# Rotary queries of the latent attention: products and turnings between the latent queries and among the first attention blocks

## The chip, the cores and the metric

One core of a Trainium2 chip runs one program. The metric is the device time of one execution in microseconds (us), the median over the runs of a kernel. TensorE is called PE in the profile (its weight loads PEld), VectorE DVE, ScalarE ACT, GpSimd POOL and SyncE SP. Each engine works off its own instructions in order, and they meet through semaphores.

## The reference, cut to what matters

The program is one step of a two-layer decoder trunk for 512 prompt tokens and 8 sample tokens. Layer 0 mixes tokens by sliding-window attention and retention, layer 1 by multi-head latent attention; behind each stand a cross-attention into 256 memory tokens and a mixture of experts. The change touches layer 1's latent attention alone:

```python
def mla_project(x, pos, w_in, q_norm, kv_norm, w_uq, w_uk):
    cq, ckv, kr = jnp.split(x @ w_in, [MLA_Q_RANK, MLA_Q_RANK + MLA_KV_RANK], axis=-1)
    cq = rms_norm(cq, q_norm)
    ckv = rms_norm(ckv, kv_norm)
    kr = rope(kr[:, :, None, :], pos)[:, :, 0]
    q = (cq @ w_uq).reshape(B, S, MLA_HEADS, MLA_NOPE + MLA_ROPE)      # 8 heads, 64 + 32
    q_nope, q_rope = jnp.split(q, [MLA_NOPE], axis=-1)
    q_rope = rope(q_rope, pos)
    q_lat = jnp.einsum('bshn,chn->bshc', q_nope, w_uk)                 # 128 per head
...
def mla_attend(q_lat, q_rope, rows, mask):
    s = einsum('bqhc,bkc->bhqk', q_lat, ckv) + einsum('bqhr,bkr->bhqk', q_rope, kr)
    s = jnp.where(mask, s * ((MLA_NOPE + MLA_ROPE) ** -0.5), NEG_INF)
    p = jax.nn.softmax(s, axis=-1)
    return jnp.einsum('bhqk,bkc->bqhc', p, ckv)
```

## The kernel before, in words

The 520 tokens are five tiles of rows: four of 128 prompt tokens, and the 8 sample tokens as tile 4. Layer 1's latent attention is `latent_attention`, which stands once for each engine (PE line 1737, ACT 2316, DVE 3099).

PSUM is cut into four pairs of banks, and all that PE makes goes through them. `psum_jobs` (line 257) writes the order of all jobs out by hand; job n uses pair n modulo 4. `open_` makes PE wait until the job four places earlier has been read out (`free`); `close` tells the reader that a job is full, `full` waits for that, and `taken` waits until a job has been read out. So every job that is put into the order shifts which earlier readout each later job waits for.

The jobs of the stretch are these. `qn` j: the plain queries of two heads by feature (line 1776), read out by DVE (even j) or ACT (odd j). `qrope` t: the rotary part of all heads for tile t (line 1793, four matmul records); DVE turns it by position in `rotate` (lines 3113 to 3118, and 3121, 3122 for tile 4), which reads PSUM with its first three instructions. `qrT` t: PE turns the rotated tile back to features (line 1803; line 1806 for tile 4), and ACT reads it out (line 1986, the helper `copy`) into `qrT2`, or for tile 4 with four small copies. `ql` h: the latent query of head h over all 520 tokens (line 1059), read out by DVE (even h) or ACT (odd h).

The order before is `qrope` 0, `ql` 0 to 7, then `qrope` 1, `qrT` 0, `qrope` 2, `qrT` 1, and so on to `qrT` 4. PE then waits until `qrT` 4 and `ql` 6 and 7 have been read out, and starts the attention.

Attention runs in 16 blocks: block i is prompt tile i // 4 (keys 128 times (i // 4 + 1)) and two heads. Each block has three PSUM jobs: S, the scores (lines 1830 and 1833), T, the probabilities turned (line 1082), and O, the probabilities times the latents (line 1840). `latent_steps` (line 156) gives PE's order S0, S1, then S(i+2), T(i), O(i-1). DVE's order is the maxima of block i+1 (lines 2494, 2495, 2502), then the scaling of the probabilities of block i (2513, 2516), then, from block 6 on, an unrelated piece on `x` (3142). ACT's order is the exponentials of block i+1 (2097), then the readouts of T(i) and O(i-1) (1986). T(i) needs the scaled probabilities of block i; O(i) needs T(i) read out. Sample tokens have their own attention behind block 15: it begins with 16 transposes (line 1852) of cached pages that SP and POOL have loaded meanwhile (lines 657, 658).

Of the kernel before, what the change touches and what calls it, by code (L numbers as in the profile page):

```python
# [34 lines left out]
NT = 5  # L35
# [30 lines left out]
def tile_cols(t):  # L66
    return slice(t * P, t * P + ROWS[t])
# [177 lines left out]
LATENT_PE = [*LATENT_IN[:-2], ("qn", 0), ("oinT", 3), ("qn", 1), ("oinT", 4)]  # L245


LATENT_GROUPS = [slice(0, P), slice(P, 2 * P), slice(2 * P, 3 * P), slice(3 * P, 416)]
LATENT_ROWS = {2: [0], 3: [1], 4: [2, 3, 4]}
LAST_TILES = [4, 0, 1, 2, 3]  # L250
# [6 lines left out]
def psum_jobs():  # L257

    jobs = []
    jobs += [("xT", -1, t) for t in range(NT)]  # L260
    jobs += [("qa", j) for j in range(4)] + [("ka",), ("va",)]
    jobs += [("kaTok",), ("qr", 0)]
    for step, i in sliding_steps(len(SWA_BLOCKS)):
        jobs += SWA_WEAVE[i] if step == "W" else [("swa" + step, i)]
    jobs += SWA_SAMPLE
    for n in range(4):
        jobs += [("retS", n), ("retK", n)] + RET_WEAVE.get(("K", n), [])
        jobs += [("retO", n), ("retU", n)] + RET_WEAVE.get(("U", n), [])
        if n:
            jobs += [("retG", n - 1)]  # L270
    for l in range(DEPTH):
        if l == 1:
            jobs += LATENT_PE
            jobs += [("qn", j) for j in (2, 3)]
            jobs += [("qrope", 0)]
            jobs += [("ql", h) for h in range(8)]
            for t in range(NT):
                jobs += ([("qrope", t)] if t else []) + ([("qrT", t - 1)] if t else [])
            jobs += [("qrT", 4)]
            jobs += [("mla" + s, i) for s, i in latent_steps(len(MLA_BLOCKS))]  # L280
            jobs += [("pkT", 0), ("pkT", 1), ("pN",)] + [key for key in PAGE_PE if key[0] != "row"]
            jobs += [("uv", j) for j in range(4)]
        jobs += [memory_job(l, *key) for key in MEM_PE[l] if key[0] != "ms2" and (key[0] != "rt" or key == ("rt", 0))]
        if l == 0:
            jobs += [("memF", 1, 0), ("memF", 1, 1), ("rank", 0), ("mkv", 1, 0), ("table", 0), ("mkv", 1, 1)]
        else:
            jobs += [("rank", 1), ("table", 1)]
        for s, b in block_order():
            jobs += [("moe" + s, l, b)] + ([("mkT", 1)] if (l, s, b) == (0, "H", 0) else [])
    jobs += [("cmb", t) for t in LAST_TILES]  # L290
    return jobs


def decoder_step(nc, io, outs):
# [78 lines left out]
    with ExitStack() as ctx:  # L373
# [217 lines left out]
        def pair(key):  # L591
            return PS[:, J[key] % 4, :]
# [10 lines left out]
        def taken(eng, key):  # L603

            n = J[key]
            eng.wait_ge(pair_free[n % 4], n // 4 + 1)
# [421 lines left out]
        def _(pe):  # L1028
# [708 lines left out]
            def latent_attention():  # L1737
# [51 lines left out]
                def q_rope(t):  # L1789
                    key = ("qrope", t)  # L1790
                    o = open_(key)
                    for k in range(2):
                        mm = pe.matmul(o[0:ROWS[t], 0:256], cqT[:, k, tile_cols(t)], uq[:, k, 512:768],
                                       start=(k == 0), stop=(k == 1))
                    close(mm, key)

                def q_rope_back(t):
                    key = ("qrT", t)
                    o = open_(key)
                    pe.wait_ge(s["qrtok_ready"], t + 1)  # L1800
                    if t < 4:
                        for c in range(2):
                            mm = pe.transpose(o[:, c * P:c * P + P], qr_tok[:, t % 2, c * P:c * P + P], ident[:, :])
                    else:
                        for h in range(8):
                            mm = pe.transpose(o[:, 8 * h:8 * h + 8], qr_rep[0:8, h, :], ident[0:8, 0:8])
                    close(mm, key)

                q_rope(0)
                taken(pe, ("ukT",))  # L1810
                taken(pe, ("qn", 2))
                taken(pe, ("qn", 3))
                for h in range(8):
                    key = ("ql", h)
                    open_(key)
                    b, c = 64 * (h % 2), h // 2
                    close(by_feature(key, lambda k: ukT[b:b + 64, c, :], lambda k: qnT[b:b + 64, c, :], 1), key)
                for t in range(1, NT):
                    q_rope(t)
                    q_rope_back(t - 1)  # L1820
                q_rope_back(4)
                taken(pe, ("qrT", 4))
                taken(pe, ("ql", 6))
                taken(pe, ("ql", 7))

                def score(i, o, blk):
                    n, h0, g, w = blk
                    o = o.rearrange("p (g w) -> p g w", g=g)
                    for h in range(h0, h0 + g):
                        pe.matmul(o[:, h - h0, 0:w], q_lat[:, h, n * P:n * P + P], ckvT[:, 0:w], start=True, stop=False)  # L1830
                    for h in range(h0, h0 + g):
                        b, c = 32 * (h % 4), h // 4
                        mm = pe.matmul(o[:, h - h0, 0:w], qrT2[b:b + 32, c, n * P:n * P + P], krT4[b:b + 32, 0:w],
                                       start=False, stop=True, **({"tile_position": (b, 0)} if b == 96 else {}))
                    return mm
# [4 lines left out]
                        mm = pe.matmul(o[:, 0:g * P], rows[:, c, 0:P], v[:, c, :, :], start=(c == 0), stop=(c == n))  # L1840
                    return mm

                attention("mla", score, apply, latent_steps(len(MLA_BLOCKS)))


                for signal, count in (("pages_in", SP_REQUESTS), ("late_pages_in", DB - SP_REQUESTS)):
# [137 lines left out]
        def _(act):  # L1984
# [3 lines left out]
            def take(key, dst, src):  # L1988
                full(act, key)
                free(copy(dst, src(pair(key)) if callable(src) else src), key)  # L1990
# [139 lines left out]
                    between(i + 1)  # L2130
                    outputs(i)

            def latent_blocks():
                exps, probs_turned, outputs = attention_steps("mla")
                n = len(MLA_BLOCKS)
                exps(0)
                for i in range(n):
                    if i + 1 < n:
                        exps(i + 1)
                    probs_turned(i)  # L2140
                    if i:
                        outputs(i - 1)
                outputs(n - 1)

            n_rows = [0]
# [170 lines left out]
            def latent_attention():  # L2316
# [44 lines left out]
                for h in (1, 3, 5, 7):  # L2361
                    take(("ql", h), halves(q_lat[:, h, :]), halves)
                for t in range(4):
                    take(("qrT", t), qrT2[:, :, tile_cols(t)], lambda o: o[:, 0:256].rearrange("p (c q) -> p c q", c=2))

                taken(act, ("ql", 6))
                taken(act, ("ql", 7))
                act.wait_ge(s["qrS_zero"], 1)
                copy(qlS[:, :, 0:8], q_lat[:, :, 512:520].rearrange("p h b -> p b h"))
                full(act, ("qrT", 4))  # L2370
                for q in range(4):
                    ins = copy(qrS[32 * q:32 * q + 32, q, :, 0:8], pair(("qrT", 4))[32 * q:32 * q + 32, 0:64].rearrange("p (h b) -> p b h", h=8))
                free(ins, ("qrT", 4))

                act.wait_ge(s["moe_done"], 1)
                latent_blocks()
# [48 lines left out]
        def _(dve):  # L2425
# [673 lines left out]
            def latent_attention():  # L3099
# [31 lines left out]
                rotate(0)  # L3131
                for h in (0, 2, 4, 6):
                    take(("ql", h), halves(q_lat[:, h, :]), halves(pair(("ql", h))))
                for t in range(1, NT):
                    rotate(t)
                def gains(i):
                    if i == GAIN_BLOCKS:
                        dve.wait_ge(s["ln_in"], 32 * 3)
                    if i >= GAIN_BLOCKS:
                        t, c = divmod(i - GAIN_BLOCKS, 2)  # L3140
                        xt = x[0:ROWS[t], t, :]
                        ins = dve.tensor_tensor(xt, xt, lnb[0:ROWS[t], c, :], (ALU.mult, ALU.add)[c])
                        if c:
                            ins.then_inc(s["x_ready"], 1)
                        else:
                            link(ins)
# [93 lines left out]
```

## Time and profile before

| | us |
|---|---|
| median of 3 runs | 1076.29 |
| lowest and highest | 1073.14, 1077.27 |
| the profiled execution | 1078.72 |
| its span | 1077.1 |
| PE busy | 973.2 (90%) |
| DVE, ACT, POOL busy | 525.6, 353.5, 254.1 |
| mean granted TensorE clock | 0.941 |

The profiled execution is 1.62 us longer than its span and 2.43 us above the median of the three runs. Durations below are of that one execution. PEclk in the profile is the granted clock of TensorE as a share of full speed; it has two levels, 0.50 (1.2 GHz) and 1.00 (2.4 GHz), and a stretch that holds both shows a value between. A matmul's record includes its way through the array, so records overlap, and what one costs PE is better read from start to start, or in the chain of waits, which cuts the overlap off.

### The profile page before, as it was taken

The numbers are of one execution on the slowest core, as the hardware profiler recorded it, in microseconds if no ns is written. First come the engines' busy times: TensorE is split into PE (matmuls) and PEld (weight loads), VectorE is DVE, ScalarE is ACT, GpSimd is POOL, SyncE is SP. The second block draws the span as 40 slices with busy tenths as digits, with TensorE's granted clock in tenths as the row PEclk, the third lists the DMA queues.
The fourth block names the chain that finished last, engine by engine and source line by source line (L and its number), as shares of the span: only waits on it lengthen the run. The fifth ranks groups of instructions, "written<-read, shape, count | busy, mean of one in ns | idle before, by whom it ended". The sixth has DMA issues, their size and how long they took to land.

```text
span 1077.1 us, 17831 instructions
## 1 busy us (share of the span) xinstructions
PE 973.2 (90%) x6998; PEld 602.9 (56%) x6998; DVE 525.6 (49%) x1070; ACT 353.5 (33%) x879; POOL 254.1 (24%) x281
## 2 busy tenths in 40 slices
PE   7978999998999998899999298899799986999995
PEld 6866788887445857633333166657548663333332
DVE  0345630466648667243223464685268673433327
ACT  2325432120001523333333243455314342333423
POOL 2220710042500001445410115600000015362121
PEclk9998999989899998999999699899999986999998
DMA  9422361172206244989998603441056136999978
GB/s 324 108 91 46 89 198 37 42 197 78 69 0 163 79 196 152 400 298 414 415 407 336 223 1 72 100 136 61 21 175 274 40 133 215 334 398 402 417 234 196
DMA packets 81612, 203.73 MB, mean 189 GB/s; under 512 B 22682, under 2 KB 47938, under 8 KB 72432
## 3 DMA queue, kind: packets, MB, share of 16 engines
q1 hardware_dynamic: 61568, 153.44, 39.5%
q0 software_dynamic: 19952, 49.05, 14.8%
q8 instruction: 60, 0.98, 0.4%
q14 instruction: 32, 0.26, 0.1%
HBM read 184.46 MB, written 25.92 MB: 195 GB/s over the span
## 4 chain that ended last, share of the span: by engine, by line
PE 75%; DVE 11%; DMA 6%; ACT 4%; issue 3%; POOL 1%; SPq 0%; DVEq 0%; POOLq 0%; ACTq 0%
PE PS L1613 14%; PE PS L1421 11%; PE PS L1059 9%; PE PS L1160 6%; PE PS L1628 5%; PE PS L1444 3%; PE PS L1124 3%; PE PS L1047 2%; ACT arena L1986 2%; DMA x<-y_tok 2%; PE PS L1082 2%; PE PS L1830 2%; DMA arena<-in_moe_w_in_dram 2%; PE PS L1755 2%; PE PS L1840 2%
## 5 line engine op out<-in xcount | busy, mean ns | idle before, releaser
L1986 ACT ACTIVATE arena<-PS 32x520 f32<-32x520 f32 (+9 forms) x150 | 74.0, 505 | 188.0 <-PE PS L1059 42.4
L1613 PE MATMUL PS<-ring,arena 128*32 128x512 f32 x648 | 116.9, 592 | 2.9 <-DMA arena<-in_moe_w_in_dram 1.5
L1613 PE MATMUL PS<-arena 128*32 128x512 f32 x648 | 111.1, 602 | 2.9 <-issue 1.8
L1059 PE MATMUL PS<-xT,ring 128*128 128x260 f32 x416 | 94.6, 388 | 3.1 <-DVE arena L2455 2.3
L3048 DVE COPY arena<-PS 128x256 f32<-128x256 f32 x24 | 10.2, 425 | 171.6 <-PE PS L1621 171.6
L1059 PEld LDWEIGHTS PS<-xT,ring 128*128 128x128 f32 x416 | 79.0, 192 | 18.0 <-DVE arena L2455 4.3
L826 POOL TENSOR_TENSOR rstd<-rstd,small 128x1 f32<-128x1 f32 (+1 forms) x25 | 16.3, 652 | 272.4 <-DVE rstd L2743 245.3
L2263 ACT ACTIVATE arena<-PS,lnc 128x128 f32<-128x128 f32 x192 | 69.6, 470 | 22.9 <-PE PS L1602 22.9
L1628 PE MATMUL PS<-ring,arena 128*32 128x512 f32 x432 | 69.0, 595 | 1.2 <-DVE arena L3048 1.2
L1160 PE MATMUL PS<-ring,xT 128*128 128x256 f32 (+2 forms) x336 | 65.1, 354 | 0.0
L1047 PE MATMUL PS<-ident,x 128*128 128x128 f32 (+1 forms) x240 | 39.2, 318 | 28.0 <-DVE x L2819 20.0
L1613 PEld LDWEIGHTS PS<-arena 128*32 128x32 f32 x648 | 30.4, 111 | 60.4 <-issue 56.3
L864 POOL DMA_INDIRECT y_tok<-arena,slot_dest x22 | 22.3, 1014 | 174.4 <-ACT arena L2291 168.5
L1160 PEld LDWEIGHTS PS<-ring,xT 128*128 128x128 f32 (+1 forms) x336 | 57.0, 186 | 7.0
L1613 PEld LDWEIGHTS PS<-ring,arena 128*32 128x32 f32 x648 | 31.5, 110 | 48.8 <-issue 44.6
L1421 PE MATMUL PS<-ring,xT 128*128 128x512 f32 x128 | 56.8, 593 | 0.7 <-ACT xT L1986 0.7
L2281 ACT ACTIVATE arena<-PS 128x256 f32<-128x256 f32 x24 | 9.3, 386 | 142.9 <-PE PS L1613 142.9
L1995 ACT ACTIVATE xT<-PS,lnc 128x128 f32<-128x128 f32 (+1 forms) x100 | 37.7, 438 | 54.7 <-PE PS L1047 35.6
L1047 PEld LDWEIGHTS PS<-ident,x 128*128 128x128 f32 (+1 forms) x240 | 35.0, 202 | 36.8 <-issue 33.3
L1613 PE MATMUL PS<-xT,arena 128*32 128x512 f32 x240 | 50.3, 593 | 0.8 <-DVE arena L3032 0.8
L1421 PE MATMUL PS<-ring,arena 128*128 128x512 f32 x96 | 48.1, 643 | 2.1 <-issue 2.1
L2097 ACT ACTIVATE pbuf<-PS,negmax 128x256 f32<-128x256 f32 (+3 forms) x96 | 45.1, 481 | 10.7 <-DVE negmax L2502 10.6
(433 smaller groups left out, 1867.9 us busy)
## 6 DMA issues: line engine op xcount, KB each, us to landing
arena<-in_moe_w_in_dram SPq DMA_DIRECT2D x27, 1024.0 KB
ring<-in_moe_w_in_dram SPq DMA_DIRECT2D x27, 1024.0 KB
ring<-in_moe_w_out_dram SPq DMA_DIRECT2D x18, 1024.0 KB
ring<-in_w_in_even_dram SPq DMA_DIRECT2D x11, 1024.0 KB
xT<-in_moe_w_in_dram SPq DMA_DIRECT2D x10, 1024.0 KB
arena<-in_moe_w_out_dram SPq DMA_DIRECT2D x8, 1024.0 KB
xT<-in_moe_w_out_dram SPq DMA_DIRECT2D x6, 1024.0 KB
y_tok<-in_c_zeros_dram POOLq DMA_DIRECT2D x8, 512.0 KB, 10.6
```

Of the source, the lines that this page charges most:

```text
L1047: mm = pe.transpose(o[:, chunk_cols(k, r)], by_k[:, k, :], ident[0:r, 0:r])
L1059: mm = pe.matmul(o[out_rows, 512 * h:512 * h + HALF], lhs(k), rhs(k)[:, HALF * h:HALF * h + HALF], start=(k == 0), stop=(k == nk - 1))
L1124: mm = pe.matmul(o[:, 512 * c:512 * c + 256], memF[l][:, k, m * P:m * P + P], wview(("m" + w, l))[:, k, :], start=(k == 0), stop=(k == KD ...
L1160: mm = pe.matmul(o[0:ROWS[t], n * width:n * width + width], xT[:, k, tile_cols(t)], w[:, k, cols], start=(k == 0), stop=(k == KD - 1))
L1421: mm = pe.matmul(o[0:ROWS[t], 512 * h:512 * h + 512], out_part(i, 2 * n + k, t), w[:, k, 512 * h:512 * h + 512], start=(n == 0 and k == 0) ...
L1444: mm = pe.matmul(o[:, j * r:j * r + r], w[:, k, j * P:j * P + P], xT[:, k, tile_cols(t)], start=(k == 0), stop=(k == KD - 1))
L1613: mm = pe.matmul(o[group(q), 0:512], xT_[:, k, group(q)], w(q, k), start=(k == 0), stop=(k == KD - 1), **quarter(q))
L1628: mm = pe.matmul(o[group(q), 512 * h:512 * h + 512], a[:, c, group(q)], w(q)[:, c, 512 * h:512 * h + 512], start=(c == 0), stop=(c == 1), ...
L1986: return act.activation(dst, src, ACT.Copy)
L1995: ins = act.activation(dst(k), src(k), ACT.Identity, scale=lnc[:, i, 0, k:k + 1], bias=lnc[:, i, 1, k:k + 1])
L2097: ins = act.activation(prob_view(kind, i)[:, h, :], score_view(kind, i)[:, h, :], ACT.Exp, bias=negmax[:, n % 2, h:h + 1], scale=SCALE[kin ...
L2263: ins = act.activation(dst[:, k, :], o[:, k * P:k * P + P], ACT.Identity, scale=lnc[:, 3 * l + 1, 0, k:k + 1], bias=lnc[:, 3 * l + 1, 1, k ...
```

## The change

PE, DVE and ACT get a new order by hand, and the order of PSUM jobs follows it. `qrope` 1, `qrT` 0, `qrope` 2 and `qrT` 1 stand between the `ql` jobs. `qrope` 3 stands behind S1, `qrT` 2 behind S2, `qrope` 4 (the sample rows) behind O0, `qrT` 3 behind O1, and `qrT` 4 behind O3. DVE rotates tile 3 behind the scaling of block 0 and tile 4 behind that of block 2. ACT reads out `qrT` 2, 3 and 4 at the end of its blocks 0, 2 and 4. A block waits for the `qrT` of its own tile where that tile's first block begins, and no longer for `qrT` 4. The work itself is the same, instruction for instruction.

```diff
+LATENT_QUERY = keys("qrope.0 ql.0 ql.1 qrope.1 ql.2 ql.3 qrT.0 ql.4 ql.5 qrope.2 qrT.1 ql.6 ql.7")
+LATENT_QUERY_DVE = keys("rot.0 ql.0 ql.2 rot.1 ql.4 rot.2 ql.6")
+LATENT_QUERY_ACT = keys("ql.1 ql.3 qrT.0 ql.5 qrT.1 ql.7")
+MLA_WEAVE = {("S", 1): [("qrope", 3)], ("S", 2): [("qrT", 2)], ("O", 0): [("qrope", 4)], ("O", 1): [("qrT", 3)], ("O", 3): [("qrT", 4)]}
+MLA_WEAVE_DVE = {0: 3, 2: 4}
+MLA_WEAVE_ACT = {0: 2, 2: 3, 4: 4}
...
-            jobs += [("qrope", 0)]
-            jobs += [("ql", h) for h in range(8)]
-            for t in range(NT):
-                jobs += ([("qrope", t)] if t else []) + ([("qrT", t - 1)] if t else [])
-            jobs += [("qrT", 4)]
-            jobs += [("mla" + s, i) for s, i in latent_steps(len(MLA_BLOCKS))]
+            jobs += LATENT_QUERY
+            for s, i in latent_steps(len(MLA_BLOCKS)):
+                jobs += [("mla" + s, i)] + MLA_WEAVE.get((s, i), [])
...
-                for t in range(1, NT):
-                    q_rope(t)
-                    q_rope_back(t - 1)
-                q_rope_back(4)
-                taken(pe, ("qrT", 4))
+                for key in LATENT_QUERY:
+                    if key == ("ql", 0):
...
+                    steps[key[0]](*key[1:])
                 taken(pe, ("ql", 6))
                 taken(pe, ("ql", 7))
...
+                    if h0 == 0:
+                        taken(pe, ("qrT", n))
...
+                for st_, i in latent_steps(len(MLA_BLOCKS)):
+                    mla[st_](i)
+                    for key in MLA_WEAVE.get((st_, i), []):
+                        steps[key[0]](*key[1:])
...
+                latent_blocks(lambda i: turned_queries(MLA_WEAVE_ACT[i]) if i in MLA_WEAVE_ACT else None)
...
                 def gains(i):
+                    if i in MLA_WEAVE_DVE:
+                        rotate(MLA_WEAVE_DVE[i])
```

## Rows read from the trace of the kernel before

**Rows 1.** The page, part 1: busy time of each engine over the whole span.

```profile
PE 973.2 (90%) x6998; PEld 602.9 (56%) x6998; DVE 525.6 (49%) x1070; ACT 353.5 (33%) x879; POOL 254.1 (24%) x281
```

**Rows 2.** Chain that ended last, 600 to 780 us: start us, us, what.

```profile
664.35 0.86 PE PS L1793 x4
665.24 4.08 PE PS L1059 x32
...
675.93 0.69 DVE arena L3122
...
677.43 0.21 ACT decay L1986
...
678.38 1.22 PE PS L1830 x4
...
687.79 0.87 PE PS L1830 x4
688.66 0.66 PE PS L1833 x4
...
690.74 1.03 ACT pbuf L2097 x4
...
741.99 1.75 PE PS L1852 x16
```

**Rows 3.** Stretches on PE: us, PE busy (x), PEclk, DMA share, GB/s.

```profile
656.00:661.00 5.00, 4.26 (x16) 0.66 0.47 111
674.00:678.00 4.00, 1.64 (x13) 0.93 0.38 87
678.00:687.00 9.00, 8.62 (x37) 0.50 0.47 98
740.00:750.00 10.00, 10.00 (x86) 1.00 0.28 92
755.00:759.00 4.00, 2.32 (x47) 1.00 0.00 0
```

**Rows 4.** Timeline of PE: start us, us, engine line op, tiles xcount [idle before <-releaser].

```profile
682.14 1.22 PE L1830 MATMUL PS<-arena 128*128 128x128 f32 x4
683.29 0.80 PE L1833 MATMUL PS<-arena 32*128 32x128 f32 x4
684.08 0.66 PE L1082 MATMUL PS<-ident,pbuf 128*128 128x128 f32 x2
684.53 1.06 PE L1830 MATMUL PS<-arena 128*128 128x128 f32 x4
...
689.22 0.44 PE L1082 MATMUL PS<-ident,pbuf 128*128 128x128 f32 x2
689.50 0.60 PE L1840 MATMUL PS<-pT,arena 128*128 128x256 f32 x2
689.93 1.03 PE L1830 MATMUL PS<-arena 128*128 128x256 f32 x4
```

**Rows 5.** Timeline of DVE, the same columns.

```profile
671.81 0.42 DVE L3113 TENSOR_TENSOR arena<-PS,rope_t 128x256 f32<-128x256 f32 x1
...
672.66 0.43 DVE L3118 TENSOR_TENSOR arena<-arena 128x256 f32<-128x256 f32 x1
...
684.14 0.43 DVE L2494 TENSOR_TENSOR PS<-PS,band 128x256 f32<-128x256 f32 x1 [0.20 <-PE PS L1833]
...
685.33 0.48 DVE L2516 TENSOR_SCALAR pbuf<-pbuf,rowsum 128x128 f32<-128x128 f32 x2
...
692.11 0.69 DVE L2495 TENSOR_REDUCE rowmax<-PS 128x2 f32<-128x512 f32 x1
```

**Rows 6.** Timeline of ACT, the same columns.

```profile
683.38 0.37 ACT L2097 ACTIVATE pbuf<-PS,negmax 128x128 f32<-128x128 f32 x1 [1.01 <-DVE negmax L2502]
...
684.00 0.20 ACT L2097 ACTIVATION_READ_ACCUMULATOR pbuf<-PS,negmax 128x1 f32 x1
```

**Rows 7.** Timeline of SP, its DMA queue.

```profile
718.69 0.33 SPq L658 DMA_DIRECT2D xT<-in_cache_mla_dram  x1
```

More of the change, by code:

```diff
@@ L1807, in q_rope_back, with query_latents @@
                     close(mm, key)
[L1809 to L1813, printed above, removed]
+                def query_latents(h):
                     key = ("ql", h)
@@ L1817, in latent_attention @@
                     close(by_feature(key, lambda k: ukT[b:b + 64, c, :], lambda k: qnT[b:b + 64, c, :], 1), key)
-                for t in range(1, NT):
-                    q_rope(t)
-                    q_rope_back(t - 1)
-                q_rope_back(4)
-                taken(pe, ("qrT", 4))
+                steps = {"qrope": q_rope, "qrT": q_rope_back, "ql": query_latents}
+                for key in LATENT_QUERY:
+                    if key == ("ql", 0):
+                        taken(pe, ("ukT",))
+                        taken(pe, ("qn", 2))
+                        taken(pe, ("qn", 3))
+                    steps[key[0]](*key[1:])
                 taken(pe, ("ql", 6))
@@ L1841, in apply @@
                     return mm
-                attention("mla", score, apply, latent_steps(len(MLA_BLOCKS)))
+                mla = attention_steps("mla", score, apply)
+                for st_, i in latent_steps(len(MLA_BLOCKS)):
+                    mla[st_](i)
+                    for key in MLA_WEAVE.get((st_, i), []):
+                        steps[key[0]](*key[1:])
                 for signal, count in (("pages_in", SP_REQUESTS), ("late_pages_in", DB - SP_REQUESTS)):
@@ L2131, in sliding_attention, with latent_blocks @@
                     outputs(i)
-            def latent_blocks():
+            def latent_blocks(between):
                 exps, probs_turned, outputs = attention_steps("mla")
@@ L2142, in latent_blocks @@
                         outputs(i - 1)
+                    between(i)
                 outputs(n - 1)
@@ L2360, in latent_attention, with turned_queries @@
                     take(("qn", j), halves(qnT[:, j, :]), halves)
[L2361 to L2373, printed above, removed]
+                def turned_queries(t):
+                    if t < 4:
+                        take(("qrT", t), qrT2[:, :, tile_cols(t)], lambda o: o[:, 0:256].rearrange("p (c q) -> p c q", c=2))
+                        return
+                    act.wait_ge(s["qrS_zero"], 1)
+                    full(act, ("qrT", 4))
+                    for q in range(4):
+                        ins = copy(qrS[32 * q:32 * q + 32, q, :, 0:8], pair(("qrT", 4))[32 * q:32 * q + 32, 0:64].rearrange("p (h b) -> p b h", h=8))
+                    free(ins, ("qrT", 4))
+                    taken(act, ("ql", 6))
+                    taken(act, ("ql", 7))
+                    copy(qlS[:, :, 0:8], q_lat[:, :, 512:520].rearrange("p h b -> p b h"))
+                for what, n in LATENT_QUERY_ACT:
+                    if what == "qrT":
+                        turned_queries(n)
+                    else:
+                        take(("ql", n), halves(q_lat[:, n, :]), halves)
                 act.wait_ge(s["moe_done"], 1)
-                latent_blocks()
+                latent_blocks(lambda i: turned_queries(MLA_WEAVE_ACT[i]) if i in MLA_WEAVE_ACT else None)
                 for g in range(2):
@@ L3130, in latent_attention @@
                     take(("qn", j), halves(qnT[:, j, :]), halves(pair(("qn", j))))
[L3131 to L3135, printed above, removed]
+                for what, n in LATENT_QUERY_DVE:
+                    if what == "rot":
+                        rotate(n)
+                    else:
+                        take(("ql", n), halves(q_lat[:, n, :]), halves(pair(("ql", n))))
                 def gains(i):
+                    if i in MLA_WEAVE_DVE:
+                        rotate(MLA_WEAVE_DVE[i])
                     if i == GAIN_BLOCKS:
```

## The prediction, made before the changed kernel was run

> **What bounds the kernel.** I read four views, from coarse to fine. Part 1 of the page says which engine fills the span: PE is busy for 90% of it [rows 1], so what counts is PE's own work and the holes in it. The chain of waits says where the edited stretch lies and who releases whom. It runs from the first rotary product at about 664.3 to the first transpose of the sample attention at 741.99 [rows 2], 77.7 us, and nearly all of it is PE. The exception stands ahead of the first block: the eight latent-query products take 4.08 us from 665.24 to 669.3, yet block 0's scores start only at 678.38. The last links are DVE's copy for the sample rows at 675.93, their turning, and ACT's four small copies from 677.43 [rows 2]. The stretches say what that did to the clock: in 674 to 678 PE was busy for 1.64 of 4 us, and after it the granted clock was 0.50 for all of 678 to 687, with PE busy 8.62 of 9 [rows 3]. The timelines of PE, DVE and ACT give the durations of a block's steps [rows 4 to 6]. The reader is to see two costs in the old order, a hole and a slow clock behind it, and to ask what the new order pays for removing them.
>
> **What hole and clock cost now.** From 669.3 to 678.38 are 9.1 us. Four rotary products at 0.89 (one lasts from 664.35 to 665.24 [rows 2]) and some 1.5 for the five turnings are 5.1 of work, so the holes are about 4.0. Moved work costs the same wherever it goes, as PE is the bound. In the new order not all of the hole goes (below).
> At 0.50 a score job of 128 keys takes 1.94 (682.14 to 684.08) [rows 4], 1.88 in the chain's measure. No row shows it at 1.00. Half is 0.94, and a job of 256 keys at 1.00, with twice the columns, takes 1.53 (0.87 and 0.66) [rows 2]; between these I take 1.0, as the columns halve too. Four such jobs then lose 3.5. Two T jobs lose 0.17 each (0.45 against 0.28 from start to start, 684.08 and 689.22 [rows 4]), O0 some 0.4 (0.43 at full clock [rows 4], taken to double), the start of S4 0.1. The slow clock costs 4.4.
> On that price there is a figure in the Trainium skill, TensorE: Matmul & The Clock Gate, section Back-to-back issue gap: about 81 ns for a weight load and matmul of 128 columns at full clock. An estimate by it is 0.65 for the eight records of such a score job, and the result would fall by some 0.3 us. No row here shows that job at full clock.
>
> **What the new order adds.** I walked the three engines through the new order with the rows' durations, each waiting for what the semaphores name, and did so first for the old order: it ended within 0.1 us of the trace. Durations: score 1.0 (128 keys) and 1.53 (256); DVE's maxima and scaling of one block 1.67 (684.14 to 685.81), 0.3 more for 256 keys because the maximum takes 0.69 [rows 5]; exponentials 0.82 (683.38 to 684.20 [rows 6]) and 1.03 [rows 2]; a rotation 1.28 (671.81 to 673.09 [rows 5]), of which PSUM is free after 0.84, and 0.68 more for tile 4 (the copy at 675.93 lasts 0.69 [rows 2]); ACT's copies for the sample rows 0.95 (677.43 to 678.38 [rows 2]) and one more for the sample latents.
> Between the latent queries PE waits twice, 0.8 each. `ql` 4 needs the pair of `qrope` 1, which DVE reads behind `ql` 0 and `ql` 2. S0 needs `ql` 6, which DVE copies behind the rotation of tile 2. So S0 starts at about 673.2 instead of 678.4, with two rotary products and three turnings still to do. Of the 4.0 of holes 1.6 stay: a gain of 2.4. The walk of the old order had only 3.5 of them, since it lets records follow without the small gaps; by it the gain is 1.9, and I take that, the two walks being alike in this.
> Inside the attention the four pairs of PSUM decide. Before, a score job opened when a T or O job was read out. The five added jobs shift this by one place each, and for a while a job has to wait for the exponentials of the latest scores:
> T1 opens when S2 is read out. DVE does the rotation of tile 3 ahead of the maxima of block 2 (its `rotate` is queued behind the scaling of block 0), so scaling 1 and exponentials 2 end near 680.2. PE is done with S3 at 678.9: 1.4 idle.
> S4 needs S3's exponentials, queued on ACT behind T1 and O0: 0.4, partly under `qrope` 4.
> S5 needs S4's exponentials. DVE is in the rotation of tile 4 (1.9 with its copy) until 683.9, then the maxima (1.3), then ACT 1.0: 686.4. PE has only T2, O1 and `qrT` 3 to do meanwhile: 1.6 idle. Here the wait for the sample rows comes back that stood ahead of block 0 before.
> T4: 0.4. S7 needs S6's exponentials, and ACT does T4, O3 and the sample rows' copies first, until 693.3; the exponentials end at 694.3, PE has been idle since 691.9: 2.4.
> With 0.2 at S3 the sum is 6.3, against 0.5 in the same blocks of the old order. From S7 on the pairs fall back into the old pattern, and blocks 8 to 15 cost what they cost.
> The sum, with the clock at 1.00 throughout: minus 1.9, minus 4.4, plus 5.8 is minus 0.5 us.
>
> **Queues it moves past.** Nothing moves on SP or POOL. The last cached page is requested at 718.69 [rows 7], over 20 us before 742, so an attention shorter by some us still doesn't wait for pages. The slot of the rotary weights is released some 15 us later than before, but its next load comes behind the sample attention. DVE's pieces on `x` begin at block 6, behind both rotations. All of these I cost at nothing.
>
> **The clock is the open term.** In 674 to 678 PE was busy 1.64 of 4 us, and the clock fell; in 755 to 759 it was busy 2.32 of 4 and the clock stayed at 1.00 [rows 3]. The new order has no hole as long as the old one but three of 1.4 to 2.4 us close together. Around S7 PE is idle for 2.8 of 4 us, which is nearer to the row where it fell. A single fall is short in this trace: within 656 to 661 the mean of 0.66 makes it 3.4 of the 5 us at 0.50 [rows 3]. If 3.4 us run at half speed, up to half is lost: the walk gives 0.6 where the loss hides under the next hole and 1.9 where it does not, 1.3 in the middle. Added to minus 0.5 that is plus 0.8.
>
> **The rivals.**
> A, the forecast: the holes come as walked and the clock falls once. Plus 0.8 (plus 0.1 to 1.4). Chance 0.45.
> B: the holes come, the clock holds, as at 755 to 759. Minus 0.5. Chance 0.22.
> C: it falls twice, at S5's hole and at S7's. The walk gives 3.5 on minus 0.5: plus 3.0. Chance 0.14.
> D, slower: it falls at T1's hole near 680.5 and doesn't come back before S7, as it stayed low from 678 to 687 though PE was busy [rows 3]. All the work from T1 to S6 runs at half speed, some 6.5 us more: plus 6.1. It decides from the point where the clock is low at S4 and the hole before S5 keeps it low. For it: the stretch holds the same short jobs. Against it: 256-key jobs are denser, and at 687 it came back among them. Chance 0.10. A rule of the Trainium skill speaks for it, same page, section Part 4: PE-mode transpose: the clock's rise doesn't engage for transposes, which don't count as busy in the same way; T and `qrT` jobs would then be holes too. The trace speaks against that rule here, since 740 to 750, mostly transposes, ran at 1.00 [rows 3].
> E, faster: the change does less harm than the pairs' order says, as the exponentials end before PE asks (reads overlap more than the rows let me see). Then the 5.8 shrink towards nothing and the result is minus 6.3. Against it: the old order's walk, with the same durations, fits. Chance 0.05.
> The rest, 0.04, is for a shift further down that none of these name.
>
> **How the numbers follow.** The profiled execution would take 1078.72 + 0.8 = 1079.5. The median of the runs before is 2.4 below that execution, so the time is 1076.29 + 0.8 = 1077.1. The runs of before spread from 3.2 below to 1.0 above their median. For 8 in 10 I take B with that spread downwards, 1076.29 - 0.5 - 2.8 = 1073.0, and C with half its way to D upwards, 1081.5. A measurement of this kernel tells 0.5%, 5.4 us, from no change. A, B and C lie within it, D beyond with some spread of C, E beyond on the other side: faster 0.05, within 0.83, slower 0.12.
>
> **What would show it.** Right: S0 near 673; PE waiting for ACT's exponentials (line 2097) ahead of S5 and S7 by 1.6 and 2.4, and ahead of T1 for DVE or ACT by 1.4; the granted clock at 1.00 from 670 to 680; the first transpose at line 1852 within 1.5 of 742. The forecast is wrong if S7's hole is under 1, if the clock is at 0.50 for more than one short stretch between 673 and 700, or if blocks 8 to 15 take another time than before.

## The result, and the profile after

The kernel before took 1076.2 us (median of 8 runs, 1073.14 to 1081.98), the changed one 1082.95 us (median of 8 runs, 1081.54 to 1087.2). The ratio is 1.0065 with a 95% interval of 1.0047 to 1.0082, so the change costs some 6.8 us (7.0 by the ratio). The forecast was plus 0.8 (no change that can be told), with a range up to 1081.5; the change is slower by a little over the bound of 0.5%, and by more than the range. The profiled execution of the changed kernel took 1087.2 us, its span 1085.5; that of before had a span of 1077.1.

Part 1 of the changed kernel's page answers to [rows 1]. The span grew by 8.4 us, PE's busy time by 3.0 with the same number of records: a part is dearer records, the rest idle time.

```profile
PE 976.2 (90%) x6998; PEld 601.6 (55%) x6998; DVE 524.8 (48%) x1070; ACT 352.1 (32%) x879; POOL 253.4 (23%) x281
```

Next the chain that ended last, of the changed kernel (start us, us, what), which answers to [rows 2]. Its lines are shifted: the rotary products are L1796, the scores L1834 and L1837, the exponentials L2105, the page transposes L1860.

```profile
666.31 0.86 PE PS L1796 x4
...
676.32 0.70 PE PS L1834 x4
...
682.47 0.81 ACT pbuf L2105 x4
...
690.09 1.03 ACT pbuf L2105 x4
...
698.46 1.03 ACT pbuf L2105 x4
...
749.75 1.75 PE PS L1860 x16
```

Before, too, the chain left PE for exponentials behind the start of block 0 (at 690.74 [rows 2], for one), but PE was idle for at most 0.42 us at any such place. Now it leaves PE ahead of T1 (683.33), S5 (691.17) and S7 (699.54), the three places that the walk had named, with PE idle for 1.2 to 2.4 us. PE's timeline gives their size (idle time and what ended it in brackets at the end of a line):

```profile
672.01 1.15 PE L1062 MATMUL PS<-arena 64*128 64x260 f32 x8 [1.14 <-DVE arena L3129]
...
676.32 0.70 PE L1834 MATMUL PS<-arena 128*128 128x128 f32 x4 [0.79 <-DVE arena L3141]
...
677.37 0.71 PE L1834 MATMUL PS<-arena 128*128 128x128 f32 x4
...
683.33 0.69 PE L1085 MATMUL PS<-ident,pbuf 128*128 128x128 f32 x2 [1.17 <-ACT pbuf L2105]
...
691.17 1.13 PE L1834 MATMUL PS<-arena 128*128 128x256 f32 x4 [1.78 <-ACT pbuf L2105]
...
699.54 1.38 PE L1834 MATMUL PS<-arena 128*128 128x256 f32 x4 [2.41 <-ACT pbuf L2105]
```

The stretches on PE of the changed kernel (us, PE busy, PEclk, DMA share, GB/s) answer to [rows 3]:

```profile
678.00:683.00 5.00, 4.15 (x29) 1.00 0.46 103
683.00:687.00 4.00, 3.67 (x10) 0.57 0.41 101
687.00:700.00 13.00, 8.58 (x50) 1.00 0.45 100
700.00:707.00 7.00, 7.00 (x20) 0.52 0.30 64
```

The granted clock is at its upper level (1.00) where before it was at 0.50, but it falls behind T1's hole (0.57 of 4 us, so 3.4 us at the lower level) and again behind S7's (0.52 of 7, so 6.7 us), there with PE busy without a pause. Together that is about the 10 us of before.

To compare all kernels I use one stretch, from the start of the first rotary product in PE's timeline to the start of the first page transpose, and within it the starts of score jobs. "Rest" is all from that transpose to the end of the span. Before and after were profiled again later (below), so before has three traces and after two.

| | S0 after | S7 after | stretch | rest | low clock within it |
|---|---|---|---|---|---|
| before | 14.19 | 30.85 | 77.64 | 335.23 | 10.2 |
| before again | 14.18 | 31.21 | 78.00 | 336.10 | 10.2 |
| before, third | 14.18 | 30.98 | 77.73 | 333.99 | 10.2 |
| after | 10.17 | 33.39 | 83.44 | 335.94 | 3.4 and 6.8 |
| after again | 10.17 | 31.92 | 81.95 | 336.27 | 6.8 |

By the means the stretch grew by 4.9 us (82.7 against 77.8) and the rest by 1.0.

### The profile page after: what moved, and what is told of

Its sections match the earlier page's. It is cut to its first block, busy times and chain, and to the rows that moved or that the text cites. A ratio compares the mean times of both kernels' runs of the same rounds, so it can differ in the third digit from the quotient of the medians.

```text
span 1085.5 us, 17835 instructions
## 1 busy us (share of the span) xinstructions
PE 976.2 (90%) x6998; PEld 601.6 (55%) x6998; DVE 524.8 (48%) x1070; ACT 352.1 (32%) x879; POOL 253.4 (23%) x281
## 4 chain that ended last, share of the span: by engine, by line
PE 75%; DVE 12%; DMA 5%; ACT 4%; issue 3%; POOL 1%; SPq 0%; DVEq 0%; POOLq 0%; ACTq 0%
PE PS L1616 15%; PE PS L1424 11%; PE PS L1062 9%; PE PS L1163 6%; PE PS L1631 6%; PE PS L1447 3%; ACT arena L1994 2%; PE PS L1127 2%; PE PS L1050 2%; DMA arena<-in_moe_w_in_dram 2%; PE PS L1085 2%; PE PS L1758 2%; PE PS L1844 2%; PE PS L1834 2%; PE PS L1605 1%
## 5 line engine op out<-in xcount | busy, mean ns | idle before, releaser
L3062 DVE COPY arena<-PS 128x256 f32<-128x256 f32 x24 | 10.2, 425 | 172.4 <-PE PS L1624 172.4
L2105 ACT ACTIVATE pbuf<-PS,negmax 128x256 f32<-128x256 f32 (+3 forms) x96 | 44.9, 480 | 10.0 <-DVE negmax L2516 9.9
```

Source lines behind the costliest of these rows:

```text
L2105: ins = act.activation(prob_view(kind, i)[:, h, :], score_view(kind, i)[:, h, :], ACT.Exp, bias=negmax[:, n % 2, h:h + 1], scale=SCALE[kin ...
```

## The experiments

The theory to be tested had two parts: the walk through the PSUM pairs is right, so holes of the forecast size come; and the clock's fall behind them costs more than the 1.3 forecast. Its rivals: the two first traces differ by chance, as the clock may fall anywhere (R1); the early rotary products between the latent queries do the harm, not those among the blocks (R2); the holes cost by themselves, the clock little (R3). A further question is which move of the sample rows would bring what the change wanted.

**The same two kernels again.** No edit; one more execution of the changed kernel and two of before, each with its trace.

> The kernel before once more, for a second trace of the stretch from the first rotary product to the last attention block. In the first it took 77.6 us with 10.2 us at 0.50. Theory: the order and the holes are the same to 0.1 us, but where the clock is low is not, as the clock's falls in the four variants so far came at other places behind the same holes; with 3 to 7 us at 0.50 it takes 75 to 76.5. Rival: it is fixed by the program, 77.6 again.

> The kernel before a third time: with the first two traces it shows how far the stretch's length differs from execution to execution. Theory: between 75 and 78 us, by where and how long the clock is low from 677 to 690. Rival: 77.6 each time.

> The changed kernel once more, for a second trace. In the first the stretch took 83.4 us with 10.2 at 0.50, of them 6.8 behind S7's hole. Theory: holes of 1.2, 1.8 and 2.4 us ahead of T1, S5 and S7 again; between 3.4 and 14 us at 0.50, so 80 to 85 us. Rival: 83.4 again, within 0.3.

Measured: 1077.14 and 1075.01 us for before, 1082.48 for the changed kernel, beside 1076.74 (median of 17 runs of before taken with them). The stretches on PE around block 0, before again and then the third trace of before:

```profile
672.00:675.00 3.00, 0.83 (x10) 1.00 0.43 101
675.00:686.00 11.00, 10.46 (x42) 0.53 0.40 97
686.00:698.00 12.00, 11.74 (x60) 1.00 0.41 98
```

```profile
675.00:686.00 11.00, 10.15 (x42) 0.53 0.42 99
```

The low clock behind block 0's hole stays for some 10.3 us (0.53 of 11; 10.2 by finer stretches) in each of three traces, though PE is busy for over 10 of the 11 us. I had expected the other two traces of before to show a stretch of 75 to 76.5, with an earlier return of the clock; that was wrong. R1 falls for this part: the fall here is the same in all three executions. The changed kernel again, timeline and stretches of PE:

```profile
679.75 0.44 PE L1085 MATMUL PS<-ident,pbuf 128*128 128x128 f32 x2 [1.17 <-ACT pbuf L2105]
...
686.13 1.13 PE L1834 MATMUL PS<-arena 128*128 128x256 f32 x4 [1.55 <-ACT pbuf L2105]
...
694.50 1.29 PE L1834 MATMUL PS<-arena 128*128 128x256 f32 x4 [2.41 <-ACT pbuf L2105]
```

```profile
680.00:695.00 15.00, 10.61 (x58) 1.00 0.42 99
695.00:702.00 7.00, 7.00 (x19) 0.52 0.36 83
```

Same holes, same fall behind S7, but none behind T1, though its hole is 1.17 us in both traces. So the fall behind S7 comes in both traces and the one behind T1 in one of them (a kernel below has T1's hole of 1.17 us as well, and the clock holds there too); the latter cost 1.5 us (S7 after 33.39 against 31.92). From S7 to the end of the stretch both traces of the changed kernel take the same, 50.05 and 50.03, and the three of before 46.79, 46.79 and 46.75. The fall behind S7 costs 3.3 us.

**The holes filled.** Unneeded matmuls into an unused part of the open PSUM pair stand where PE would wait. Nothing of the computation is left out.

```diff
+FILLED = {("S", 3): [(("mlaT", 0), 2)], ("O", 1): [(("qrT", 3), 3)], ("O", 3): [(("qrT", 4), 4)]}
+def fill(key, n):
+    for _ in range(n):
+        pe.matmul(pair(key)[:, 512:768], ident[:, :], ckvT[:, 0:256], start=True, stop=True)
...
                         steps[key[0]](*key[1:])
+                    for key, n in FILLED.get((st_, i), []):
+                        fill(key, n)
```

A first kernel had 5, 7 and 9 of them:

> The changed kernel with 21 idle matmuls (128x256, into an unused half of a pair, their results read by nobody) in the three holes ahead of T1 (5), S5 (7) and S7 (9); at some 0.22 us each they are shorter than the holes. Theory P: the holes stay (1.2, 1.8, 2.4 us) but the clock stays at 1.00 from block 0 on; what the two falls cost in the trace (10.2 us at 0.50, some 4.5 to 5 us lost) comes back: 4 to 5 us faster than the changed kernel, +1.5 to +3 on before. A rival (the holes alone make the loss, the low clock lies under them): no gain, or a loss of 1 us, on the changed kernel: +6 to +8 on before.

It measured 1082.54 us, ratio 1.0061 (1.0041 to 1.0080), stretch 82.29. The granted clock was 1.00 throughout the attention, but one such matmul is two records and takes 0.46 us, more than I had reckoned: the 7 behind `qrT` 3 took 3.19 us and the 9 behind `qrT` 4 took 4.15, longer than their holes of 1.8 and 2.4, and S7 came at 35.62. It doesn't test the clock's price, as the filling itself delays. The second kernel has 2, 3 and 4:

> The filled changed kernel with idle matmuls of the right number: one of them is two records of PE and lasted 0.45 us in the trace of the run before, so 2, 3 and 4 of them (0.9, 1.35, 1.8 us) fit into the holes ahead of T1, S5 and S7 without making them longer. Theory P (holes and clock): the stretch from the first rotary product to the last attention block, 83.4 us in the trace of the changed kernel, falls to 78 to 79, as the 10.2 us at 0.50 cost about 5; the time is 4 to 5.5 us below the changed kernel's, +1.5 to +3 on before. Rival (the holes alone): 83, no gain.

It measured 1079.88 us (12 runs), ratio 1.0025 (1.0010 to 1.0040). PE's timeline (the fillers are L1822, the scores L1840) and its stretches:

```profile
684.92 1.46 PE L1822 MATMUL PS<-arena,ident 128*128 128x256 f32 x6
686.58 1.13 PE L1840 MATMUL PS<-arena 128*128 128x256 f32 x4 [0.20 <-ACT pbuf L2113]
...
692.47 1.99 PE L1822 MATMUL PS<-arena,ident 128*128 128x256 f32 x8
694.96 1.13 PE L1840 MATMUL PS<-arena 128*128 128x256 f32 x4 [0.49 <-ACT pbuf L2113]
```

```profile
673.00:695.00 22.00, 20.51 (x115) 1.00 0.45 97
695.00:742.00 47.00, 46.25 (x215) 1.00 0.37 116
```

The fillers leave 0.20 and 0.49 of waiting, so S5 and S7 start no later than their exponentials allow: S7 after 31.86, as in the second trace of the changed kernel (31.92). Behind S7 the clock stays up, and the stretch ends at 78.64, 46.78 behind S7, which is before's value. This separates the two costs in one pair of kernels: with the same starts of the jobs up to S7, the low clock behind S7 costs 3.3 us (81.95 to 78.64), and the new order with the clock up all the way still takes 0.9 more than the old one with its 10 us of low clock (78.64 against 77.8). So R3 falls in its second half: the clock does not cost little. The holes do cost by themselves, as forecast: 5.4 us in the first trace of the changed kernel and 5.1 in the second. The time went back by 3.1 us (1082.95 to 1079.88), by the two ratios 4.3; with the noise of both that is the 3.3.

**The early half alone.** The products and turnings stand between the latent queries as in the change, and the last five in front of block 0; none among the blocks.

```diff
-LATENT_QUERY = keys("qrope.0 ... ql.6 ql.7")
+LATENT_QUERY = keys("qrope.0 ... ql.6 ql.7 qrope.3 qrT.2 qrope.4 qrT.3 qrT.4")
-LATENT_QUERY_DVE = keys("rot.0 ... ql.6")
+LATENT_QUERY_DVE = keys("rot.0 ... ql.6 rot.3 rot.4")
-LATENT_QUERY_ACT = keys("ql.1 ... ql.7")
+LATENT_QUERY_ACT = keys("ql.1 ... ql.7 qrT.2 qrT.3 qrT.4")
+MLA_WEAVE = MLA_WEAVE_DVE = MLA_WEAVE_ACT = {}
```

> Only the first part of the change: rotary products and turnings of tiles 1 and 2 stand between the latent queries; tiles 3 and 4 stay ahead of block 0 as before, nothing among the blocks. Theory P (the woven jobs shift the four PSUM pairs, scores wait for exponentials, the clock falls in these holes): the early part alone is nearly free. The wait ahead of the sample rows' turning (1.7) and the slow clock on blocks 0 to 3 stay; the walk gives +0.4, so within -1 to +1.5 us of before. Theory W (the interleaving itself costs, by DVE's queue ahead of block 0 or in something upstream): +3 us or more, most of the change's 6.8.

Measured: 1078.33 us (12 runs), ratio 1.0019 (1.0005 to 1.0032), stretch 77.04, S0 after 14.54. The timeline of PE:

```profile
677.15 0.63 PE L1809 MATMUL PS<-ident,arena 8*128 8x8 f32 x8 [1.66 <-DVE arena L3136]
677.71 0.71 PE L1834 MATMUL PS<-arena 128*128 128x128 f32 x4
```

The early half brings S0 no earlier, since the sample rows' copy and turning (the wait of 1.66 for DVE) still end the part in front of it. It isn't the harm in the stretch either (77.04 against 77.8), so R2 falls there: what the change adds to the stretch comes from the jobs among the blocks. The low clock is there for 6.8 us instead of 10.2: it begins 2.3 us behind S0, among the short blocks, and not ahead of block 0. The kernel's time is 2.0 us above before by the ratio (0.5 to 3.4), which is more than the 1.5 that I allowed and less than theory W's 3. As the stretch is not longer, R2 stays open for what the change loses outside the stretch, and that is about as much (1.9).

**The same filling in the kernel before.** Fillers stand in front of and behind `qrT` 4, where before's PE waits 1.73 and 0.99 us.

```diff
...
+                fill(("qrT", 3), 7)
                 q_rope_back(4)
+                fill(("qrT", 4), 4)
...
```

> The kernel before with 11 idle matmuls in the hole ahead of block 0 (7 while PE waits for the sample rows' rotation, 4 while it waits for ACT's copies). Theory P prices the slow clock on blocks 0 to 4 at 4.4 us, less what the softmax chain then makes PE wait for (some 0.9 by the walk): -3 to -4.5 us on before, with the clock at 1.00 from 662 on. A rival (at full clock DVE and ACT bound the first blocks anyway): -0 to -1.5 us, with new waits ahead of T0 to T3.

Measured: 1077.35 us, ratio 1.0013 (0.9996 to 1.0030), stretch 77.82; here too the fillers were longer than the waits, and S0 came 2.0 later. The clock was not at 1.00 from 662 on, as theory P had it: it fell for 3.4 us ahead of T0. With 3 and 2 instead of 7 and 4:

> The kernel before with 3 and 2 idle matmuls (1.35 and 0.9 us) in its two waits ahead of block 0 (1.7 and 1.0). The 7 and 4 of the run before put block 0 off by 2.0 us and left the stretch at 77.8, where before has 77.6. Theory P: block 0 starts where it did (14.2 us after the first rotary product), and the stretch takes 75.5 to 76, so -1.5 to -2.5 us on before. Rival (the short jobs of blocks 0 to 3 pull the clock down whatever stands ahead of them, as it fell at 681.7 in the run before): the stretch within 1 us of 77.6, time 0 to -1.

Measured: 1075.86 us (12 runs), ratio 0.9986 (0.9970 to 1.0001), stretch 76.31. Its stretches and its timeline on PE (scores L1837 and L1840):

```profile
675.00:684.00 9.00, 7.76 (x54) 1.00 0.48 102
684.00:688.00 4.00, 3.69 (x14) 0.57 0.50 104
```

```profile
679.74 0.71 PE L1837 MATMUL PS<-arena 128*128 128x128 f32 x4
...
680.80 0.71 PE L1837 MATMUL PS<-arena 128*128 128x128 f32 x4
...
682.74 0.41 PE L1082 MATMUL PS<-ident,pbuf 128*128 128x128 f32 x2 [0.81 <-DVE pbuf L2523]
```

The 10 us of low clock shrink to 3.4, but don't vanish: the clock now holds through the hole and falls later, among the short 128-key jobs, where T0 and T1 wait 0.81 and 0.31 for DVE. Of the 4.4 that the slow clock was said to cost, 1.5 come back in the stretch (76.31 against 77.8). Jobs that PE finishes sooner wait for DVE instead; the slow clock had partly run under DVE's work. The stretch came 0.3 above theory P's 75.5 to 76 and 0.3 outside the rival's limit of 1 us from 77.6; the fall among the short jobs is what the rival said.

**Sample rows at the end of the attention.** `qrope` 4 goes behind O11 and `qrT` 4 behind O15; the rest is as in the change, but for ACT: it reads `qrT` 4 out behind the last block, after copying the sample latents, and PE waits for that ahead of the sample attention's new rows.

```diff
-MLA_WEAVE = {("S", 1): [("qrope", 3)], ("S", 2): [("qrT", 2)], ("O", 0): [("qrope", 4)], ("O", 1): [("qrT", 3)], ("O", 3): [("qrT", 4)]}
+MLA_WEAVE = {("S", 1): [("qrope", 3)], ("S", 2): [("qrT", 2)], ("O", 1): [("qrT", 3)], ("O", 11): [("qrope", 4)], ("O", 15): [("qrT", 4)]}
-MLA_WEAVE_DVE = {0: 3, 2: 4}
+MLA_WEAVE_DVE = {0: 3, 13: 4}
-MLA_WEAVE_ACT = {0: 2, 2: 3, 4: 4}
+MLA_WEAVE_ACT = {0: 2, 2: 3}
...
+                taken(pe, ("qrT", 4))
...
+                turned_last()
...
```

> The changed kernel with the sample rows alone moved on: their product behind O11, their rotation behind scaling 13, their turning and its readout behind O15 (a wait for it ahead of the new-row scores). Theory P: S5 still waits 1.6 (pair order, without the rotation in DVE's queue before it), S7's hole of 2.4 and the clock's fall behind it (3.3 lost) are gone, some 2.4 are paid at the end where PE waits for rotation and readout: 4 to 5 us faster than the changed kernel, +1.5 to +3 on before. Theory W: no difference to the changed kernel, +6 to +7.5.

Measured: 1079.22 us (12 runs), ratio 1.0024 (1.0003 to 1.0046), stretch 79.66. PE's timeline:

```profile
677.16 0.44 PE L1085 MATMUL PS<-ident,pbuf 128*128 128x128 f32 x2 [1.17 <-ACT pbuf L2106]
...
682.05 1.76 PE L1834 MATMUL PS<-arena 128*128 128x256 f32 x4 [1.50 <-ACT pbuf L2106]
```

S7's hole is gone with `qrT` 4, as the walk says. T1's and S5's holes stay, the clock falls for 6.8 us behind S5's instead (the first half of a score job of 256 keys takes 1.69 there, 682.05 to 683.74, where it takes 0.95 further down), and the stretch is 3.0 shorter than the changed kernel's mean. So S7's hole came from the sample rows, and those ahead of T1 and S5 stand with `qrope` 3, `qrT` 2 and `qrT` 3 alone among the blocks.

**Sample rows first.** `qrope` 4 is the first rotary product, all turnings stand between the latent queries, and no job stands among the blocks.

```diff
+LATENT_QUERY = keys("qrope.4 ql.0 ql.1 qrope.0 ql.2 ql.3 qrT.4 qrope.1 ql.4 qrT.0 qrope.2 ql.5 qrT.1 qrope.3 ql.6 ql.7 qrT.2 qrT.3")
+LATENT_QUERY_DVE = keys("rot.4 ql.0 rot.0 rot.1 rot.2 rot.3 ql.6")
+LATENT_QUERY_ACT = keys("ql.1 ql.2 ql.3 qrT.4 ql.4 qrT.0 ql.5 qrT.1 ql.7 qrT.2 qrT.3 qls.0")
+MLA_WEAVE = MLA_WEAVE_DVE = MLA_WEAVE_ACT = {}
...
```

> No rotary work among the attention blocks. The sample rows' product comes first, so that their long rotation lies under latent queries; tiles 0 to 3 follow, interleaved with the latent queries, which ACT reads out for the greater part (6 of 8, before 4); the sample rows' rotated copy lies in a part of the buffer of the turned probabilities. By the walk PE waits 0.3 ahead of block 0, which starts 11.1 us after the first rotary product (before 14.2), and no score waits for exponentials: 73 to 75 us for the stretch at 0 to 7 us of slow clock, so -2.5 to -4.5 us on before. Rival (the interleaving's cost is in DVE's queue, as in the run with the early part alone, +2.0): block 0 starts at 13 or later, time 0 to +2.

Measured: 1076.89 us (12 runs), ratio 1.0000 (0.9983 to 1.0017), stretch 75.61. The part in front of block 0 runs on PE almost without a wait:

```profile
677.31 0.86 PE L1807 MATMUL PS<-ident,arena 128*128 128x128 f32 x4
678.48 0.68 PE L1835 MATMUL PS<-arena 128*128 128x128 f32 x4 [0.31 <-DVE arena L3143]
```

S0 comes after 13.29, not after the 11.1 that my walk gave: the work itself is longer than I summed. Two `ql` take 1.08 and a product 1.06 in this mixed order. The clock falls once for 3.4 us among the short blocks. The stretch wins 2.2 us, the median nothing. That is the outcome of the rival (S0 at 13 or later, time 0 to +2), but not its reason: DVE's queue makes PE wait only 0.3 ahead of block 0.

**Sample rows inside the last two blocks.** The prompt's products and turnings stand between the latent queries; `qrope` 4 goes behind T14 and `qrT` 4 behind T15, under DVE's and ACT's work for the last blocks. Here too PE waits for `qrT` 4 ahead of the sample attention's new rows.

```diff
+LATENT_QUERY = keys("qrope.0 ql.0 ql.1 qrope.1 ql.2 ql.3 qrT.0 qrope.2 ql.4 ql.5 qrT.1 qrope.3 ql.6 ql.7 qrT.2 qrT.3")
+LATENT_QUERY_DVE = keys("rot.0 ql.0 rot.1 ql.2 rot.2 rot.3 ql.6")
+LATENT_QUERY_ACT = keys("ql.1 ql.3 qrT.0 ql.4 ql.5 qrT.1 ql.7 qrT.2 qrT.3")
+MLA_WEAVE = {("T", 14): [("qrope", 4)], ("T", 15): [("qrT", 4)]}
+MLA_WEAVE_DVE = {15: 4}
+MLA_WEAVE_ACT = {15: 4}
...
```

> The sample rows behind T14 and T15, where the attention ends and no score job comes after them; tiles 0 to 3 ahead of block 0, interleaved. By the walk block 0 starts 9.4 us after the first rotary product, scores wait for nothing new, and the sample rows cost 1.0 of waits at the end: 72 to 75 us for the stretch, -2.5 to -5 us on before. If the loss of the change lay in the interleaving and not in the order of PSUM pairs among the blocks, it would be +1 or more.

Measured: 1074.98 us (12 runs), ratio 0.9992 (0.9974 to 1.0011), stretch 72.32, S0 after 10.09. The stretch came as forecast, the time did not: it can't be told from before. The granted clock is 1.00 through the whole stretch, with no filler in it, although PE waits 0.82 and 0.31 for DVE ahead of T0 and T1. From S0 to S7, with the same jobs as in before, PE takes 13.74 us, where before takes 16.8 as the mean of three traces: the 10 us of low clock there cost 3.1 net, or 4.2 without these two waits, which before doesn't have. The 4.4 of my sum was about right. The same kernel with one filler behind S2:

```diff
+FILLED = {("S", 2): [(("qrT", 3), 1)]}
```

> The kernel with the sample rows behind T14 and T15 and one idle matmul (0.45 us) in the 0.8 us that PE waits ahead of T0. It keeps the clock at 1.00 through the short jobs of blocks 0 to 3 if idleness there is what lets it fall. The stretch took 72.3 us without it in the one trace, and 72.3 again is expected. Theory: on the clock what is gained in the stretch reaches the end, 2 to 5 us below before (0.2 to 0.5%). Rival: half or more of it is lost behind the stretch, as the one trace of its sibling shows (5.3 gained, 0.5 left); then 0 to 1.5 us below before.

Measured: 1074.58 us (12 runs, 1072.69 to 1076.96) against 1076.74, ratio 0.9975 (0.9959 to 0.9991), stretch 72.35. This is the lowest median of the study; the kernel is faster than before and than the changed one, but it can't be told from the one without the filler, nor did the filler do anything for the clock, which was at 1.00 without it. Its stretches on PE:

```profile
664.00:674.00 10.00, 9.96 (x59) 1.00 0.42 96
674.00:698.00 24.00, 22.93 (x127) 1.00 0.43 97
698.00:737.00 39.00, 38.25 (x182) 1.00 0.42 134
760.00:767.00 7.00, 6.85 (x78) 0.52 0.01 2
838.00:845.00 7.00, 7.00 (x30) 0.53 0.32 91
```

PE is busy 9.96 of 10 us in front of block 0 and the clock stays at 1.00 through the whole attention: 5.4 us less than before in the stretch. But the median gives 2.2 and the ratio 2.7, half of it. The theory's 2 to 5 us hold, and so does the rival's half that is lost, but not its 0 to 1.5. The rest takes 337.77, against 335.1 as the mean of before. Its last two rows show the likely place: 6.7 and 6.6 us of low clock. The kernel before has 0.83 in each of the 10 us around the same work, which is 3.4 each:

```profile
764.00:774.00 10.00, 7.85 (x145) 0.83 0.01 2
842.00:852.00 10.00, 10.00 (x38) 0.83 0.30 107
```

In the chain of waits the 32 products of one line take 5.26 us in the kernel without the filler (first line, from 836.03) and 3.71 before:

```profile
836.03 5.26 PE PS L1447 x32
```

```profile
840.15 3.71 PE PS L1444 x32
```

That the longer low stretches eat the missing 2.7 is read from these rows; no run tests it, nor why they are longer. The mean granted clock of all runs speaks for it. Twice its missing share times the span is the time at the lower level: 115.2 us with the filler (before, in the same set of runs, 119.8) and 119.8 without it (before 120.8). Their stretches, in one trace each, lost all of the 10.2 us, so some 5.6 and 9.2 us of low clock came up elsewhere. At half speed that is up to 2.8 and 4.6 us, an estimate; missing are 2.7 and 4.6.

## Why the prediction was wrong, point by point

**The holes: right.** T1 1.17 (forecast 1.4), S5 1.78 and 1.55 (1.6), S7 2.41 in both traces (2.4), each for ACT's exponentials. The reason for S7's is the one given. ACT's timeline of the changed kernel shows the copies for the sample rows between O3's readout and the exponentials of block 6:

```profile
696.63 0.38 ACT L1994 ACTIVATE arena<-PS 128x256 f32<-128x256 f32 x1
697.22 0.89 ACT L1994 ACTIVATE decay<-PS 32x64 f32<-32x64 f32 x4 [0.21 <-PE PS L1809]
698.14 0.32 ACT L1994 ACTIVATE arena<-arena 128x64 f32<-128x64 f32 x1
698.46 0.47 ACT L2105 ACTIVATE pbuf<-PS,negmax 128x256 f32<-128x256 f32 x1
```

**S0: 1.2 too early.** It was forecast some 9.0 behind the first rotary product (673.2 less 664.19) and came after 10.17. The wait at `ql` 4 is 1.14 (0.8 forecast), which is 0.3. In the mixed order two `ql` take 1.08 and a product 1.06 (one of the three 0.96) from start to start, where I had taken 1.02 and 0.89 from the old order: four pairs and three products are another 0.6 to 0.7. I took the price of a product from a link of the chain [rows 2] that cuts its overlap off.

**S0 to S7: 0.6 too short.** The walk gave 21.1 (694.3 less 673.2); the trace in which the clock held until S7 gives 21.75 (31.92 less 10.17). The price of a short score job was right: 1.0 forecast, 1.05 measured (676.32 to 677.37). Of the Trainium skill, TensorE: Matmul & The Clock Gate, section Back-to-back issue gap, the estimate for it was 0.65; the trace disagrees, with eight records in 1.05 us, 0.13 each.

**The clock: the step that failed.** The forecast's term was "the clock falls once", 3.4 us long, for 1.3 us. It falls behind S7 in both traces, as rival A said, but stays low for 6.8 us and costs 3.3, since PE has no idle time there under which a part could hide. I had taken the length of a fall from the shortest one in the trace, though [rows 3] showed one of over 9 us behind the old hole with PE busy; and I kept that length only for rival D. In one of two traces the clock falls behind T1 as well, for another 1.5. The gain of the low clock of before (4.4 in my sum) was thus given back: over all runs, twice the missing share of the mean granted clock times the span is 122.0 us at the lower level in the changed kernel and 119.8 to 122.3 in before (means of three sets of 17 to 35 runs). With the three holes filled it is 113.2.

**The sum.** Minus 0.5, plus 1.2 (S0), plus 0.6 (S0 to S7), plus 3.3 (S7's fall), plus 0.75 (T1's fall, in one of two traces) is plus 5.3, where the stretch measured plus 4.9. Without any fall it would be plus 1.3; the kernel with filled holes measured plus 0.9. Rival B's minus 0.5 would have been wrong even with the clock up. Rival C, two falls and plus 3.0, is the nearest in mechanism and was too small for the same reason. Rival D's plus 6.1 (minus 0.5 and 6.5 are 6.0) is the nearest number to the measured 6.8, by luck: its mechanism, a clock that stays low from T1 to S7, was in neither trace. E didn't occur. The bounds of my range had slips of their own: half the way from C to D is plus 4.6, or 1080.8 and not 1081.5, and the spread downwards is 3.2 and not 2.8.

**Outside the stretch.** The medians differ by 6.8, the stretch by 4.9. The forecast costed all else at nothing. The rest grew by 1.0, and the traces place that: a fall of the clock some 22 to 25 us behind the stretch, after a wait of 3.46 us that every kernel has, lasts 3.4 us in all three traces of before and 6.8 in both of the changed kernel. From the first page transpose to the job behind that fall before takes 31.3 us three times (741.83 to 773.11 in its first trace), the changed kernel 32.4 and 32.5 (749.59 to 782.00). First before, then the changed kernel and its stretch there:

```profile
773.11 0.41 PE L1923 MATMUL PS<-ident,arena 128*128 128x128 f32 x2 [0.49 <-ACT arena L1986]
```

```profile
782.00 0.41 PE L1931 MATMUL PS<-ident,arena 128*128 128x128 f32 x2 [0.49 <-ACT arena L1994]
```

```profile
771.00:779.00 8.00, 5.98 (x75) 0.57 0.00 0
```

So a kernel's order in the attention comes with another length of a fall behind it; why is not shown. The part ahead of the stretch, the same work in both kernels, scattered from 661.4 to 664.2 in before and was 662.6 and 666.2 in the changed kernel; its variants with the same order up to S0 had 660.0 to 663.1. The kernels with the early half alone, with the holes filled and with the sample rows first also took 2 to 3 us more than their stretches say. What of this is not the clock stays open.

## What to carry to other kernels

When a job is put into a fixed rotation of buffers, walk the readouts again: each later job waits for another earlier reader, and that walk, by durations of the trace, gave the three long holes among the blocks within 0.25 us. Price a fall of the clock by the work that stands behind the hole, dense and with nothing idle to hide it, and by the longest fall that the trace shows behind a like hole, not the shortest. Small late work did least harm here where its consumer's engines were busy with something else anyway, right ahead of its own use: so placed, it left a stretch of 72.3 us, where before has 77.8. Then look at what the gained time turns into further down; half of it was gone at the end.

## What the runs showed of the hardware

The granted clock stayed at the lower level for 10.2 us with PE busy 10.0 to 10.5 of 11 us, in three traces of one program, and for 6.8 us with PE busy 7.00 of 7, in two traces of another. These two falls had the same length in every trace of their program; others did not, such as the first fall of before, near 76 us, which lasted 10.2, 6.8 and 10.2 us. With the same hole of 1.17 us the clock fell in one execution and held in two (the second one with the sample rows at the end). It also fell among short fp32 score jobs (128 keys, half of the records with 32 rows) behind waits of only 0.81 and 0.31 us, and held through waits of 0.82 and 0.31 at the same jobs in the kernel with the sample rows inside the last two blocks and no filler. Unneeded matmuls in three waits kept it at 1.00 and were worth 3.3 us in the stretch. An fp32 matmul of 128x256 against a 128x128 weight is two records and takes 0.46 us at full clock.
